# Trainium2 two-block network: all eight residual sums behind out-projection and MLP on VectorE, none on GpSimd

## The chip, the cores and the metric

The program runs on one core of one Trainium2 chip. The time is device microseconds of one whole execution. TensorE (PE in the profile) does the matrix products, VectorE (DVE) and ScalarE (ACT) do elementwise work, GpSimd (POOL) is a fourth engine for elementwise work, and SyncE (SP) issues the transfers. Each engine works through its own queue in order and waits on semaphores for the others.

## What is computed

A first block of two layers works on 512 latent rows and 256 context rows of width 1024, a second block of two layers works on the latent rows alone. Each layer of the first block is a token mixer (Fourier, two kinds of attention, convolution) with an output projection, and an MLP. Behind each of the two stands a gated, normalized residual:

```python
h = _modulate(x, g_pre_mix[l], sx1, cx1)
x = x + gx1 * _rms_norm(_token_mixer(h, kv_ctx, rope, lp, lam, lam_init), g_post_mix[l])
hm = _modulate(x, g_pre_mlp[l], sx2, cx2)
x = x + gx2 * _rms_norm(_sq_relu_mlp(hm, w_ff1[l], w_ff2[l]), g_post_mlp[l])

if l < DEPTH - 1:        # the context, first layer only
    xc = xc + gc1 * _rms_norm(_token_mixer(hc, kv_ctx, None, lp, lam, lam_init), g_post_mix[l])
    hcm = _modulate(xc, g_pre_mlp[l], sc2, cc2)
    xc = xc + gc2 * _rms_norm(_sq_relu_mlp(hcm, w_ff1[l], w_ff2[l]), g_post_mlp[l])
```

So there are six residuals: two of the context (256 columns) and four of the latents (512 columns). The second block has none of this form.

## The kernel before

Activations lie feature-major: `x` (or `context`) is eight tiles f = 0..7 of 128 features by NT columns, NT being 512 or 256, in float32. Every float32 product is made of three passes of split operands (`w_hi`·`h_hi`, `w_hi`·`h_lo`, `w_lo`·`h_hi`, lines 367 to 369 of `Weights.multiply`). ScalarE writes `w_hi` (line 345) and VectorE writes `w_lo` (line 353) of a weight chunk some chunks ahead of its use.

`rest_stage` is what follows the merged branches of a layer: the output projection (eight tiles, evicted to `y`), the norm of y, the residual, the norm in front of the MLP, the MLP in two turns, and again the norm and the residual. It is called for the context of layer 1, the latents of layer 1 and the latents of layer 2. No planner orders it. Each engine has a function, and its order is the order in which that function is written.

One residual (function `residual` on VectorE, line 1413) is this, for f = 0 to 7:

- VectorE scales a tile, `m[f % 4] = y[f] * gain[f] * rows` (line 1420; `m` is called `mid` in the profile, and `rows` is a bank of PSUM with the inverse root for every column).
- The tile is added to x, `x[f] += m[f % 4]`. VectorE adds the tiles 0, 2, 4, 6 and 7 (line 1424), each behind the scaling of the next tile; GpSimd adds the tiles 1, 3 and 5 (line 1403).
- ScalarE squares the new x[f] into `squares[f % 4]` (line 905, called through `RowNorm.square`) for the norm that comes next, `pre_mlp` or `following`.
- TensorE sums four squared tiles at a time (line 913, `RowNorm.sum`, called when f is 3 and when f is 7). ScalarE may square tile 4 only when the first sum is done, since the four buffers are used again.

Two counters say how far the adding is: `rest_added_dve` and `rest_added_pool`. Scaling a tile from f = 4 on waits until tile f - 4 has been added.

Before each sum TensorE runs `keep_busy` products (line 471), 128 by 128 products of constants whose results nobody reads: 32 for 512 columns and 16 for 256, in two runs, one before each sum. In the layer-1 latents' out-projection, `fill` puts products of the modulation (line 2926) in their place. After the second sum come `gather` (VectorE, line 919), `fold` (TensorE, 924), `root` (ScalarE, 930), `invert` (VectorE, 935) and `turn` (TensorE, 940). Then the first products of the MLP may start, or the next stage.

The last residual of the layer-1 context is not done in `rest_stage`. A `LateResidual` object carries it into the input stage of the latents, where its steps are woven among the others' by the marks that each thread yields (`weave_by_clock`: the step with the lowest mark comes next). Its scaling is line 1163, its adding line 1167 on VectorE and line 1174 on GpSimd.

Of the kernel before, what the change touches and what calls it, by code (L numbers as in the profile page):

```python
# [1112 lines left out]
class LateResidual:  # L1113
# [3 lines left out]
    BY_POOL, BY_DVE = (1, 3, 5), (0, 2, 4, 6, 7)  # L1117

    def __init__(self, K, x, y, m, norm, gain, NT, homes):
        self.K, self.x, self.y, self.m, self.norm, self.gain, self.NT, self.homes = K, x, y, m, norm, gain, NT, homes  # L1120
        S = K.count_of
        self.scaled, self.added = S("rest_scaled"), (S("rest_added_dve"), S("rest_added_pool"))

    def wait_added(self, eng, f):
        if f in self.BY_POOL:
            eng.wait_ge(self.added[1].sem, self.added[1].at(self.BY_POOL.index(f) + 1))
        else:
            eng.wait_ge(self.added[0].sem, self.added[0].at(self.BY_DVE.index(f) + 1))

    def wait_all(self, eng):  # L1130
        self.wait_added(eng, self.BY_POOL[-1])
        self.wait_added(eng, self.BY_DVE[-1])
# [17 lines left out]
    def dve(self, dve):  # L1150
# [5 lines left out]
        for f in range(KD + 1):  # L1156
# [8 lines left out]
            if f - 1 in self.BY_DVE:  # L1165
                dve.wait_ge(self.scaled.sem, self.scaled.at(f))
                nc.vector.tensor_tensor(self.x[:, f - 1, 0:NT], self.x[:, f - 1, 0:NT], m[:, (f - 1) % 4], ALU.add)\
                    .then_inc(self.added[0].sem, 1)

    def pool(self, pool):  # L1170
        for f in self.BY_POOL:
            yield 1.0 + 0.15 * f
            pool.wait_ge(self.scaled.sem, self.scaled.at(f + 1))
            self.K.nc.gpsimd.tensor_tensor(self.x[:, f, 0:self.NT], self.x[:, f, 0:self.NT], self.m[:, f % 4], ALU.add)\
                .then_inc(self.added[1].sem, 1)

    def close(self):
        self.norm.close()
        self.scaled.advance(KD)
        self.added[0].advance(len(self.BY_DVE))  # L1180
        self.added[1].advance(len(self.BY_POOL))
# [4 lines left out]
def rest_stage(K, x, merged, mod, mods, NT, following, gates, h, kept, M=None, homes=(), fetch=None, side=None):  # L1186
# [7 lines left out]
    scaled, added = S("rest_scaled"), (S("rest_added_dve"), S("rest_added_pool"))  # L1194
# [13 lines left out]
    with ExitStack() as scope, K.block() as block:  # L1208
# [55 lines left out]
        by_pool = (1, 3, 5)  # L1264
        by_dve = (0, 2, 4, 6, 7)

        def wait_added(eng, turn, f):
            if f in by_pool:
                eng.wait_ge(added[1].sem, added[1].at(len(by_pool) * turn + by_pool.index(f) + 1))
            else:  # L1270
                eng.wait_ge(added[0].sem, added[0].at(len(by_dve) * turn + by_dve.index(f) + 1))
# [126 lines left out]
        @block.gpsimd  # L1398
        def _(pool):
            def residual(turn):  # L1400
                for f in by_pool:
                    pool.wait_ge(scaled.sem, scaled.at(KD * turn + f + 1))
                    nc.gpsimd.tensor_tensor(x[:, f, 0:NT], x[:, f, 0:NT], m[:, f % 4], ALU.add).then_inc(added[1].sem, 1)

            wait_x(pool)
            residual(0)
            if side is None:
                residual(1)

        @block.vector  # L1410
        def _(dve):
            def residual(norm, gain, turn):
# [3 lines left out]
                for f in range(KD + 1):  # L1416
# [5 lines left out]
                    if f - 1 in by_dve:  # L1422
                        dve.wait_ge(scaled.sem, scaled.at(KD * turn + f))
                        nc.vector.tensor_tensor(x[:, f - 1, 0:NT], x[:, f - 1, 0:NT], m[:, (f - 1) % 4], ALU.add)\
                            .then_inc(added[0].sem, 1)
# [7 lines left out]
            wait_added(dve, 0, by_pool[-1])  # L1433
            wait_added(dve, 0, by_dve[-1])
# [32 lines left out]
            if side is None:  # L1467
                residual(post_mlp, mods[:, 3], 1)
                wait_added(dve, 1, by_pool[-1])
# [4 lines left out]
    for s, n in ((scaled, residuals * KD), (added[0], residuals * len(by_dve)), (added[1], residuals * len(by_pool)),  # L1474
# [1298 lines left out]
def input_stage(K, lead, vec, lam, NT, kv, branch, rstd, rope, dft, late=None, late_transfer=None):  # L2773
# [8 lines left out]
    with ExitStack() as scope, K.block() as block:  # L2782
# [79 lines left out]
        def _(pool):  # L2862
            more = [late.pool(pool)] if late is not None else []
            weave_by_clock(fourier.pool(pool), *more)
# [1493 lines left out]
```

## Time and profile before

| | |
|---|---|
| median of 3 runs | 3651.61 us (3648.67 to 3653.59) |
| the profiled execution | 3650.45 us |
| its span, first to last instruction | 3648.7 us |
| TensorE busy | 3458.3 us, 95% |
| VectorE busy | 1906.9 us, 52% |
| ScalarE busy | 1394.7 us, 38% |
| GpSimd busy | 72.5 us, 2% |
| mean granted TensorE clock | 0.978 |

The profiled execution lies 1.16 us below the median, and 1.75 us of it lie outside the span. A busy share is a mean over stages with different limits. What the change meets is six short stretches, which begin at about 382, 591, 1233, 1636, 2359 and 2735 us of the span.

### The profile page before, as it was taken

Reading aid. Unit: us, or ns where it says so; the run is one execution under the profiler, and the core shown is the slowest. Engines: PE = TensorE matmul, PEld = TensorE weight load, DVE = VectorE, ACT = ScalarE, POOL = GpSimd, SP = SyncE. Lnnn points to the kernel's source line nnn. Section 1 sums busy time; section 2 is a strip of 40 time slices with the busy share of each in tenths; the row PEclk is TensorE's granted clock in tenths of the full one; section 3 lists DMA queues with packets and bytes.
Section 4 is the critical chain, followed back from the end, with each engine's and each line's share of the span. In section 5 each row is a group of like instructions: output and inputs, shape, how many; then the busy total and the mean of one; then the engine's idle time right before and its main releaser. Section 6 shows DMA issues by size and latency. Waiting matters only on the chain. (4 is left out here: it accounts for less than half of the span.)

```text
span 3648.7 us, 46697 instructions
## 1 busy us (share of the span) xinstructions
PE 3458.3 (95%) x18528; PEld 2716.4 (74%) x18528; DVE 1906.9 (52%) x3008; ACT 1394.7 (38%) x2383; POOL 72.5 (2%) x58
## 2 busy tenths in 40 slices
PE   7999999999999999998999999999997999989999
PEld 5878898765777677877775677788876776667767
DVE  4655677856544433444856544354443365333653
ACT  4544443344443422224334443322223444343442
POOL 0000000000000000000000000000000000000000
PEclk8999999999999999998999999999998999999999
DMA  5555454211123643323221122223332211222112
GB/s 194 196 192 196 145 185 148 72 56 41 58 64 110 237 164 119 98 87 113 76 70 41 47 67 96 81 82 98 98 93 78 74 60 41 88 92 70 58 41 98
DMA packets 97260, 366.73 MB, mean 101 GB/s; under 512 B 11168, under 2 KB 11424, under 8 KB 95520
## 3 DMA queue, kind: packets, MB, share of 16 engines
q1 hardware_dynamic: 97056, 363.84, 31.0%
q8 instruction: 148, 2.42, 0.3%
q14 instruction: 56, 0.46, 0.0%
HBM read 354.36 MB, written 9.44 MB: 100 GB/s over the span
## 5 line engine op out<-in xcount | busy, mean ns | idle before, releaser
L353 DVE TENSOR_TENSOR w_lo<-w_raw,w_hi 128x1024 fp32r<-128x1024 f32 x545 | 667.7, 1226 | 611.5 <-ACT w_hi L345 611.3
L367 PE MATMUL banks<-h_hi,w_hi 128*128 128x512 f32 (+2 forms) x2040 | 805.6, 395 | 19.4 <-DVE h_lo L1018 6.6
L369 PE MATMUL banks<-h_hi,w_lo 128*128 128x512 f32 (+2 forms) x2040 | 747.8, 367 | 0.0
L368 PE MATMUL banks<-h_lo,w_hi 128*128 128x512 f32 (+2 forms) x2040 | 746.6, 366 | 0.0
L345 ACT ACTIVATE w_hi<-w_raw 128x1024 fp32r<-128x1024 f32 x545 | 573.4, 1054 | 311.0 <-DMA w_raw<-in_stream 299.2
L367 PEld LDWEIGHTS banks<-h_hi,w_hi 128*128 128x128 f32 (+1 forms) x2040 | 392.3, 192 | 123.4 <-issue 53.1
L369 PEld LDWEIGHTS banks<-h_hi,w_lo 128*128 128x128 f32 (+1 forms) x2040 | 390.9, 192 | 64.6
L368 PEld LDWEIGHTS banks<-h_lo,w_hi 128*128 128x128 f32 (+1 forms) x2040 | 392.8, 193 | 58.5 <-issue 10.6
L367 PE MATMUL banks<-merged_hi,w_hi 128*128 128x512 f32 (+1 forms) x960 | 341.1, 355 | 5.0 <-DVE mid L1449 2.3
L369 PE MATMUL banks<-merged_hi,w_lo 128*128 128x512 f32 (+1 forms) x960 | 337.6, 352 | 0.0
L368 PE MATMUL banks<-merged_lo,w_hi 128*128 128x512 f32 (+1 forms) x960 | 337.6, 352 | 0.0
L367 PE MATMUL banks<-mid_hi,w_hi 128*128 128x512 f32 (+1 forms) x768 | 273.8, 356 | 0.5 <-DVE y L1466 0.2
L368 PE MATMUL banks<-mid_lo,w_hi 128*128 128x512 f32 (+1 forms) x768 | 271.6, 354 | 0.0
L369 PE MATMUL banks<-mid_hi,w_lo 128*128 128x512 f32 (+1 forms) x768 | 271.6, 354 | 0.0
L367 PEld LDWEIGHTS banks<-merged_hi,w_hi 128*128 128x128 f32 x960 | 180.2, 188 | 42.8 <-DVE mid L1449 5.9
L1644 ACT ACTIVATE turned<-banks 128x512 f32<-128x512 f32 (+1 forms) x176 | 96.8, 550 | 282.5 <-PE banks L1623 282.5
L369 PEld LDWEIGHTS banks<-merged_hi,w_lo 128*128 128x128 f32 x960 | 180.3, 188 | 25.3
L368 PEld LDWEIGHTS banks<-merged_lo,w_hi 128*128 128x128 f32 x960 | 180.3, 188 | 24.1
L1386 ACT ACTIVATE mid_hi<-mid 128x512 fp32r<-128x512 f32 (+1 forms) x96 | 54.0, 563 | 319.1 <-DVE mid L1449 319.0
L2416 DVE SCALAR_TENSOR_TENSOR branch<-conv_in,vectors,branch 128x512 f32<-128x512 f32 (+1 forms) x270 | 168.2, 671 | 0.2
L367 PEld LDWEIGHTS banks<-mid_hi,w_hi 128*128 128x128 f32 x768 | 145.1, 189 | 30.8 <-issue 4.6
L369 PEld LDWEIGHTS banks<-mid_hi,w_lo 128*128 128x128 f32 x768 | 145.1, 189 | 20.0
(385 smaller groups left out, 4644.2 us busy)
## 6 DMA issues: line engine op xcount, KB each, us to landing
w_raw<-in_stream SPq DMA_DIRECT2D x545, 512.0 KB, 3.6
mod_cells<-in_stream SPq DMA_DIRECT2D x48, 512.0 KB, 5.6
mod_cell<-in_stream SPq DMA_DIRECT2D x48, 512.0 KB, 5.5
x_kept<-x SPq DMA_DIRECT2D x3, 2048.0 KB, 7.2
x<-x_kept SPq DMA_DIRECT2D x3, 2048.0 KB, 8.9
x<-in_x SPq DMA_DIRECT2D x2, 2048.0 KB, 9.7
out_x<-x SPq DMA_DIRECT2D x8, 256.0 KB, 4.5
dft_table<-in_dft SPq DMA_DIRECT2D x2, 768.0 KB, 7.1
```

What stands on the lines that cost most here:

```text
L345: self.nc.scalar.activation(self.hi[:, c], self.raw[:, c], ACT.Copy).then_inc(self.hi_ready, 1)
L353: self.nc.vector.tensor_tensor(self.lo[:, c], self.raw[:, c], self.hi[:, c].bitcast(F32), ALU.subtract)\
L367: self.nc.tensor.matmul(out, w_hi, x_hi, start=start, stop=False)
L368: self.nc.tensor.matmul(out, w_hi, x_lo, start=False, stop=False)
L369: mm = self.nc.tensor.matmul(out, w_lo, x_hi, start=False, stop=stop)
L1386: nc.scalar.activation(mid_hi[:, t], m[:, t % 2], ACT.Copy).then_inc(mid_hi_ready.sem, 1)
L1644: nc.scalar.activation(self.T[:, lane:lane + lanes, a:b, i * P:(i + 1) * P], K.ps[:, 4, 0:lanes * (b - a) * P].rearrange("p (l k n) -> p l ...
L2416: nc.vector.scalar_tensor_tensor(out=self.out[:, c], in0=src, scalar=w, in1=self.out[:, c], op0=ALU.mult, op1=ALU.add).then_inc(self.done. ...
```

## The change

The division of the tiles between the two engines goes. VectorE adds each of the eight tiles, still behind the scaling of the next one. GpSimd's function in `rest_stage` and `LateResidual.pool` go, and one counter is left, `rest_added_dve`. The counts of products, of scalings, of squares and of `keep_busy` products stay, as do their orders.

```diff
-    BY_POOL, BY_DVE = (1, 3, 5), (0, 2, 4, 6, 7)
...
     def wait_added(self, eng, f):
-        if f in self.BY_POOL:
-            eng.wait_ge(self.added[1].sem, self.added[1].at(self.BY_POOL.index(f) + 1))
-        else:
-            eng.wait_ge(self.added[0].sem, self.added[0].at(self.BY_DVE.index(f) + 1))
+        eng.wait_ge(self.added.sem, self.added.at(f + 1))
...
-        @block.gpsimd
-        def _(pool):
-            def residual(turn):
-                for f in by_pool:
-                    pool.wait_ge(scaled.sem, scaled.at(KD * turn + f + 1))
-                    nc.gpsimd.tensor_tensor(x[:, f, 0:NT], x[:, f, 0:NT], m[:, f % 4], ALU.add).then_inc(added[1].sem, 1)
...
-                    if f - 1 in by_dve:
+                    if f >= 1:
                         dve.wait_ge(scaled.sem, scaled.at(KD * turn + f))
                         nc.vector.tensor_tensor(x[:, f - 1, 0:NT], x[:, f - 1, 0:NT], m[:, (f - 1) % 4], ALU.add)\
-                            .then_inc(added[0].sem, 1)
+                            .then_inc(added.sem, 1)
...
             if side is None:
                 residual(post_mlp, mods[:, 3], 1)
-                wait_added(dve, 1, by_pool[-1])
             if following is not None:
                 following.gather(dve)
```

VectorE's queue at the residual behind the out-projection of layer 2 (512 columns; `mid` is m), before:

```order
L1420 SCALAR_TENSOR_TENSOR mid_20607<-y_20604,mods_60,banks 128x512 [waits post_mix_turned]
L1420 SCALAR_TENSOR_TENSOR mid_20607<-y_20604,mods_60,banks 128x512
L1424 TENSOR_TENSOR x_20602<-x_20602,mid_20607 128x512 [waits rest_scaled]
L1420 SCALAR_TENSOR_TENSOR mid_20607<-y_20604,mods_60,banks 128x512 x2
L1424 TENSOR_TENSOR x_20602<-x_20602,mid_20607 128x512 [waits rest_scaled]
L1420 SCALAR_TENSOR_TENSOR mid_20607<-y_20604,mods_60,banks 128x512 [waits rest_added_dve]
L1420 SCALAR_TENSOR_TENSOR mid_20607<-y_20604,mods_60,banks 128x512 [waits rest_added_pool]
```

and with the change:

```order
L1388 SCALAR_TENSOR_TENSOR mid_20596<-y_20593,mods_60,banks 128x512 [waits post_mix_turned]
L1388 SCALAR_TENSOR_TENSOR mid_20596<-y_20593,mods_60,banks 128x512
L1392 TENSOR_TENSOR x_20591<-x_20591,mid_20596 128x512 [waits rest_scaled]
L1388 SCALAR_TENSOR_TENSOR mid_20596<-y_20593,mods_60,banks 128x512
L1392 TENSOR_TENSOR x_20591<-x_20591,mid_20596 128x512 [waits rest_scaled]
L1388 SCALAR_TENSOR_TENSOR mid_20596<-y_20593,mods_60,banks 128x512
L1392 TENSOR_TENSOR x_20591<-x_20591,mid_20596 128x512 [waits rest_scaled]
L1388 SCALAR_TENSOR_TENSOR mid_20596<-y_20593,mods_60,banks 128x512 [waits rest_added_dve]
L1392 TENSOR_TENSOR x_20591<-x_20591,mid_20596 128x512 [waits rest_scaled]
```

The last row shown is the add of tile 3. It was GpSimd's, and needed only the scaling of tile 3 and GpSimd's own add of tile 1. It now stands on VectorE behind five scalings and three adds.

VectorE's queue at the late residual of the context (256 columns), inside the input stage of the latents, before:

```order
L1167 TENSOR_TENSOR context_65<-context_65,mid_4009 128x256 [waits rest_scaled]
L1163 SCALAR_TENSOR_TENSOR mid_4009<-y_4005,mods_60,banks 128x256
L353 TENSOR_TENSOR w_lo_51<-w_raw_49,w_hi_50 128x1024 [waits w_hi_ready]
L1163 SCALAR_TENSOR_TENSOR mid_4009<-y_4005,mods_60,banks 128x256
L1167 TENSOR_TENSOR context_65<-context_65,mid_4009 128x256 [waits rest_scaled]
```

and with the change:

```order
L1161 TENSOR_TENSOR context_65<-context_65,mid_4009 128x256 [waits rest_scaled]
L1157 SCALAR_TENSOR_TENSOR mid_4009<-y_4005,mods_60,banks 128x256
L1161 TENSOR_TENSOR context_65<-context_65,mid_4009 128x256 [waits rest_scaled]
L353 TENSOR_TENSOR w_lo_51<-w_raw_49,w_hi_50 128x1024 [waits w_hi_ready]
L1157 SCALAR_TENSOR_TENSOR mid_4009<-y_4005,mods_60,banks 128x256
L1161 TENSOR_TENSOR context_65<-context_65,mid_4009 128x256 [waits rest_scaled]
```

One add comes in front of the split of a weight chunk (line 353), and the two others in front of the next split.

## Rows read from the trace of the kernel before

**Rows 1.** The page, busy time of TensorE and of GpSimd

```profile
PE 3458.3 (95%) x18528; PEld 2716.4 (74%) x18528; DVE 1906.9 (52%) x3008; ACT 1394.7 (38%) x2383; POOL 72.5 (2%) x58
```

**Rows 2.** Waits, layer-2 out-projection residual, 2359 to 2378 us: total, times, longest

```profile
PE banks L913 <- ACT squares L905: 2.2, 1, 2.2
...
ACT squares L905 <- POOL x L1403: 1.0, 2, 0.5
```

**Rows 3.** Timeline of ScalarE and TensorE there: start, duration, instruction, idle before

```profile
2364.60 0.63 ACT L905 ACTIVATE squares<-x 128x512 f32<-128x512 f32 x1 [0.50 <-POOL x L1403]
...
2365.28 1.07 PE L913 MATMUL banks<-squares,consts 128*32 128x512 f32 x8 [2.24 <-ACT squares L905]
2366.27 3.84 PE L471 MATMUL banks<-consts 128*128 128x128 f32 x32
2370.04 1.06 PE L913 MATMUL banks<-squares,consts 128*32 128x512 f32 x8
```

**Rows 4.** Timeline of VectorE there

```profile
2359.51 1.41 DVE L1420 SCALAR_TENSOR_TENSOR mid<-y,mods,banks 128x512 f32<-128x512 f32 x2 [1.25 <-PE banks L940]
2360.83 0.68 DVE L1424 TENSOR_TENSOR x<-x,mid 128x512 f32<-128x512 f32 x1
2361.43 1.40 DVE L1420 SCALAR_TENSOR_TENSOR mid<-y,mods,banks 128x512 f32<-128x512 f32 x2
...
2371.27 0.69 DVE L919 COPY squares<-banks 128x512 f32<-128x512 f32 x1 [3.40 <-PE banks L913]
```

**Rows 5.** Timeline of GpSimd there

```profile
2362.91 1.66 POOL L1403 TENSOR_TENSOR x<-x,mid 128x512 f32<-128x512 f32 x1 [0.26 <-DVE mid L1420]
```

**Rows 6.** Line 1424 over the run: count, ns min/median/max, first and last start

```profile
L1424 DVE TENSOR_TENSOR x<-x,mid x20: 681/683/686, 1234.6 to 2743.1; 128x512 f32<-128x512 f32 x20
```

**Rows 7.** Timeline of TensorE, first sums of the three other latent residuals

```profile
1239.03 1.07 PE L913 MATMUL banks<-squares,consts 128*32 128x512 f32 x8 [2.24 <-ACT squares L905]
...
1642.13 1.07 PE L913 MATMUL banks<-squares,consts 128*32 128x512 f32 x8 [2.24 <-ACT squares L905]
1643.13 5.47 PE L471 MATMUL banks<-consts 128*128 128x128 f32 x32
...
2741.16 1.07 PE L913 MATMUL banks<-squares,consts 128*32 128x512 f32 x8 [2.24 <-ACT squares L905]
```

**Rows 8.** Timeline of the context's out-projection residual: TensorE, VectorE, ScalarE

```profile
385.79 0.64 PE L913 MATMUL banks<-squares,consts 128*32 128x256 f32 x8 [1.67 <-ACT squares L905]
...
388.34 0.64 PE L913 MATMUL banks<-squares,consts 128*32 128x256 f32 x8
...
382.37 0.87 DVE L1420 SCALAR_TENSOR_TENSOR mid<-y,mods,banks 128x256 f32<-128x256 f32 x2 [0.80 <-PE banks L940]
383.16 0.42 DVE L1424 TENSOR_TENSOR context<-context,mid 128x256 f32<-128x256 f32 x1
383.50 0.86 DVE L1420 SCALAR_TENSOR_TENSOR mid<-y,mods,banks 128x256 f32<-128x256 f32 x2
...
385.32 0.42 ACT L905 ACTIVATE squares<-context 128x256 f32<-128x256 f32 x1 [0.17 <-POOL context L1403]
```

**Rows 9.** Timeline of VectorE at the late residual

```profile
592.78 1.37 DVE L353 TENSOR_TENSOR w_lo<-w_raw,w_hi 128x1024 fp32r<-128x1024 f32 x1
...
598.33 1.23 DVE L353 TENSOR_TENSOR w_lo<-w_raw,w_hi 128x1024 fp32r<-128x1024 f32 x1 [0.88 <-ACT w_hi L345]
```

**Rows 10.** Waits, 590 to 640 us

```profile
PEld banks L367 <- issue: 0.4, 2, 0.2
```

**Rows 11.** Stretches: length, busy PE PEld DVE ACT POOL (instructions), granted clock, DMA share, GB/s

```profile
1240.64:1244.03 3.39, 3.39 (x20) 1.22 (x20) 0.98 (x2) 0.73 (x2) 0.00 (x0) 0.50 1.04 413
1643.42:1646.83 3.41, 3.41 (x18) 3.41 (x18) 1.31 (x3) 2.10 (x4) 0.00 (x0) 0.50 0.00 0
2363.62:2367.03 3.41, 1.75 (x14) 0.91 (x15) 3.41 (x6) 1.66 (x4) 2.60 (x2) 1.00 0.00 0
...
2742.50:2745.91 3.41, 3.41 (x19) 3.41 (x18) 1.25 (x3) 2.04 (x4) 0.00 (x0) 0.50 0.01 2
```

More of the change, by code:

```diff
@@ L1121, in __init__ @@
         S = K.count_of
-        self.scaled, self.added = S("rest_scaled"), (S("rest_added_dve"), S("rest_added_pool"))
+        self.scaled, self.added = S("rest_scaled"), S("rest_added_dve")
     def wait_added(self, eng, f):
-        if f in self.BY_POOL:
-            eng.wait_ge(self.added[1].sem, self.added[1].at(self.BY_POOL.index(f) + 1))
-        else:
-            eng.wait_ge(self.added[0].sem, self.added[0].at(self.BY_DVE.index(f) + 1))
+        eng.wait_ge(self.added.sem, self.added.at(f + 1))
     def wait_all(self, eng):
-        self.wait_added(eng, self.BY_POOL[-1])
-        self.wait_added(eng, self.BY_DVE[-1])
+        self.wait_added(eng, KD - 1)
     def pe(self, pe):
@@ L1164, in dve @@
                                                op0=ALU.mult, op1=ALU.mult).then_inc(self.scaled.sem, 1)
-            if f - 1 in self.BY_DVE:
+            if f >= 1:
                 dve.wait_ge(self.scaled.sem, self.scaled.at(f))
                 nc.vector.tensor_tensor(self.x[:, f - 1, 0:NT], self.x[:, f - 1, 0:NT], m[:, (f - 1) % 4], ALU.add)\
[L1168 to L1175, printed above, removed]
+                    .then_inc(self.added.sem, 1)
     def close(self):
@@ L1179, in close @@
         self.scaled.advance(KD)
-        self.added[0].advance(len(self.BY_DVE))
-        self.added[1].advance(len(self.BY_POOL))
+        self.added.advance(KD)
         for t in self.homes:
@@ L1193, in rest_stage @@
     S = K.count_of
-    scaled, added = S("rest_scaled"), (S("rest_added_dve"), S("rest_added_pool"))
+    scaled, added = S("rest_scaled"), S("rest_added_dve")
     up_free, down_free, mid_hi_ready, mid_lo_ready = S("mlp_up_bank_free"), S("mlp_down_bank_free"), S("mlp_mid_hi"), S("mlp_mid_lo")
@@ L1262, in wait_x @@
                 eng.wait_ge(x_in.sem, x_in.at(16))
-        by_pool = (1, 3, 5)
-        by_dve = (0, 2, 4, 6, 7)
         def wait_added(eng, turn, f):
[L1268 to L1271, printed above, removed]
+            eng.wait_ge(added.sem, added.at(KD * turn + f + 1))
         beside_pe = None
@@ L1396, in _ @@
                 following.root(act)
-        @block.gpsimd
-        def _(pool):
-            def residual(turn):
-                for f in by_pool:
-                    pool.wait_ge(scaled.sem, scaled.at(KD * turn + f + 1))
-                    nc.gpsimd.tensor_tensor(x[:, f, 0:NT], x[:, f, 0:NT], m[:, f % 4], ALU.add).then_inc(added[1].sem, 1)
[L1405 to L1408, printed above, removed]
         @block.vector
@@ L1432, in _ @@
             residual(post_mix, mods[:, 1], 0)
[L1433 to L1434 removed]
+            wait_added(dve, 0, KD - 1)
             lead.dve(dve, True, range(up + AHEAD, up + SLOTS))
@@ L1473, in rest_stage @@
     residuals = 2 if side is None else 1
-    for s, n in ((scaled, residuals * KD), (added[0], residuals * len(by_dve)), (added[1], residuals * len(by_pool)),
+    for s, n in ((scaled, residuals * KD), (added, residuals * KD),
                  (K.dve_step, 8 * turns), (up_free, 8 * turns),
@@ L2862, in _ @@
         def _(pool):
-            more = [late.pool(pool)] if late is not None else []
-            weave_by_clock(fourier.pool(pool), *more)
+            weave_by_clock(fourier.pool(pool))
         @block.vector
```

1 line of the change is left out of this document (added).

## The prediction, made before the changed kernel ran

> **What bounds the kernel now.** The page comes first: TensorE is busy for 95% of the span and GpSimd for 2% [rows 1]. What lengthens the program is what lengthens TensorE's queue, so the question at each of the six residuals is whether TensorE waits there, and for whom.
>
> I read the waits of one residual, then its instructions in order of time. At the out-projection of layer 2, TensorE waits 2.24 us for ScalarE's squares before the first sum, and ScalarE waits twice for GpSimd's adds [rows 2, 3]. In order of time the chain is: GpSimd adds tile 3 from 2362.91 for 1.66 us; ScalarE squares it from 2364.60, 0.03 us after the add has ended; the sum starts at 2365.28 [rows 3, 5]. So the end of GpSimd's add of tile 3 sets the first sum. From there TensorE doesn't wait: 32 products that keep it busy run from 2366.27, and the second sum follows them at 2370.04 [rows 3]. VectorE, done with its adds by then, waits 3.40 us for that sum [rows 4]. The other three latent residuals show the same 2.24 us before their first sum [rows 7], the context's out-projection shows 1.67 us [rows 8].
>
> **VectorE's spacing.** From 2359.51 to 2360.83 there are two scalings, so one takes 0.66 us of the queue; an add takes 0.60 (2360.83 to 2361.43) and ends 0.68 after its start [rows 4]. For 256 columns the same differences give 0.395 for a scaling and 0.34 for an add, which ends 0.42 after its start [rows 8]. The changed queue alternates the same two instructions, each still one instruction behind what it needs, and the scaling of tile 4 needs the add of tile 0, long done. I let no new wait in.
>
> **First sum, four latent residuals.** The add of tile 3 now stands behind five scalings and three adds of VectorE: 5 x 0.66 + 3 x 0.60 = 5.10 us after 2359.51, that is 2364.61, and ends at 2365.29. The square then starts at 2365.32 and no longer at 2364.60: 0.72 us later. Nothing covers this, since TensorE is the one that waits; its gap grows from 2.24 to 2.96 us. Four times 0.72 is 2.88 us.
>
> **Second sum.** The added work here is three adds, 1.8 us of VectorE's queue, and it is covered. The add of tile 7 starts after 8 x 0.66 + 7 x 0.60 = 9.48 us, at 2368.99, ends at 2369.67, its square (0.63) ends at about 2370.34 and the sum could start at 2370.38. TensorE gets there by its own products at 2370.04 + 0.72 = 2370.76. The cover is 0.38 us; were it gone, each residual would cost what the adds exceed it by. The gather behind it has more: VectorE is free at 2369.67, the gather stood at 2371.27 [rows 4].
>
> **Context, out-projection.** The add of tile 3 starts 5 x 0.395 + 3 x 0.34 = 3.00 us after 382.37, ends at 385.79, and the square starts at 385.82 where it started at 385.32: 0.50 us. The second sum is a tie: TensorE's side gives 388.34 + 0.50 = 388.84, VectorE's side 382.37 + 5.54 + 0.42 + 0.42 + 0.08 = 388.83. I take 0.50, with 0.1 more as the bound.
>
> **Late residual of the context.** Three adds of 0.34 are 1.02 us more on VectorE, and behind them stand the splits of weight chunks. Before the split at 598.33 VectorE waited 0.88 us for ScalarE [rows 9], so it comes about 0.14 us late, and the one before by 0.34. The waits of this stretch hold none of TensorE's for a split, only 0.4 us of issue [rows 10]. I cost it at nothing; the cover is that weights are split chunks ahead, and all of it on the path would be 1.02 us. The transfer of the context waits for one counter instead of two and is issued long after.
>
> **GpSimd leaving.** It loses 12 adds of 1.66 us and six short ones. No queue behind them holds anything that TensorE needs at once, so this gives nothing by itself. Could VectorE have been held by GpSimd? Its 20 adds of 512 columns take 681 to 686 ns, some of them beside GpSimd's and the last two of each residual without it [rows 6], and the two scalings that run beside a GpSimd add take 1.40 us together where the two before any took 1.41 [rows 4]. I see nothing to win back in the residuals. One place looks different: the split at 592.78, while GpSimd's first late add ran, took 1.37 us and the one at 598.33 took 1.23 [rows 9]. That 0.14 us lies on a covered queue.
>
> The Trainium skill (SBUF — State Buffer, section "Who interferes with whom") says that a VectorE instruction with two SBUF inputs and a GpSimd instruction that reads SBUF exclude each other, and that the one that issues first blocks the other for its whole length. The long split agrees with it; by that rule taking GpSimd away could shorten VectorE's chain, and the sum would be smaller wherever GpSimd had come first. In the residuals the adds of 681 to 686 ns show that it didn't.
>
> **The sum.** 2.88 + 0.50 + 0 = 3.38 us on the profiled execution's 3650.45 us, or 3653.83. The median of the runs stands 1.16 higher, at 3651.61, so the forecast is 3655.0 us, 0.09% more.
>
> **The clock, the largest unknown.** In three of the four latent residuals the granted clock falls to 0.50 for about 3.4 us right behind the first sum, in the fourth it stays at 1.00, though the gap of 2.24 us is the same [rows 7, 11]. 0.50 is 1.2 GHz, 1.00 is 2.4 GHz. What a fall costs is read from the 32 products: 5.47 us with it against 3.84 without [rows 7, 3], so 1.63 us. The skill (TensorE: Matmul & The Clock Gate, Part 1) says that the gate looks at activity in windows that run freely, whatever the kernel does; the same gap with and without a fall agrees with that. What a gap of 2.96 us does no row shows.
>
> **The rivals.**
>
> (a) *The delay as summed*, 3.4 us: about 3655.0, with its own range of 3652.5 to 3657.5. For it speaks that the wait before the first sum is there five times, almost alike. Chance 0.55.
>
> (b) *The clock gives a part back.* Where the clock falls and returns at moments of its own, work that starts 0.72 us later spends 0.72 us less in the stretch of half speed, and half of the delay returns: 0.36 in three residuals, so 0.50 + 0.72 + 3 x 0.36 = 2.3 us, 3653.9. If one or two of the three falls are also missed because everything has shifted, 1.63 us go off each time: 3652.3 or 3650.6. For it speaks that one residual has no fall; against it that a longer gap makes none less likely. Chance 0.22.
>
> (c) *The clock falls in the two places where it doesn't now*, the layer-2 out-projection and the context's: 3.4 + 2 x 1.63 = 6.6 us, 3658.3. For it: the gaps grow by 0.72 and 0.50. Chance 0.14.
>
> (d) *The other side, slower by over 0.2%*: the longer gap brings half speed not for one stretch but for a second as well, at the five first sums. Each further stretch costs up to 1.63. It decides from three further stretches on, 3.4 + 4.9 = 8.3 us, 3659.9; with five it is 3.4 + 8.2 = 11.6 us, 3663.2. Against it: in all three falls seen, the clock is back when the products after the sum end. Chance 0.07.
>
> (e) *VectorE runs faster alone*, as the shared port would have it. To lose nothing at the first sum, the nine instructions up to the end of tile 3's add would have to take 5.06 us where I sum 5.78, an eighth less. Then the time stays at about 3651.6, and only a gain beyond that is faster. Chance 0.02.
>
> **How the numbers follow.** The likeliest is (a), 3655.0. The range of 3650.0 to 3661.0 holds (a), (b), (c) and the beginning of (d), and some 2 us by which the median of a few runs may lie off (the three runs shown span 4.9 us). Within 0.2%, which is 7.3 us and about what a measurement can tell from no change, lie (a), (b), (c) and (e): 0.91 after the unlikely tail of (b) and (e) below 3644.3 is taken at 0.01 or 0.02. Slower takes (d) and a corner of (c), 0.08; faster 0.01.
>
> **What would show it.** In the changed profile TensorE's wait before the first sum should be 2.9 to 3.0 us at the four latent residuals and about 2.2 at the context's, with VectorE's add of tile 3 ending 0.03 before the square. The distance from the first to the second sum should stay 4.76 us where the clock stays, and the second sum should still show no wait. VectorE's spacing should be 0.66 and 0.60. GpSimd's busy time should fall by some 25 us. I am wrong if the second sum waits for ScalarE (the cover of 0.38 was none), if the first sum isn't later (the chain was another), or if the stretches behind the first sums show a clock of 0.50 more often or longer than three times 3.4 us.

## The result

The changed kernel takes 3663.65 us (median of 9 runs, 3657.05 to 3673.28), the kernel before beside it 3655.13 us (9 runs, 3648.67 to 3656.73). The ratio is 1.0027, with a 95% interval of 1.0019 to 1.0036: slower by 7 to 13 us. A second set of 10 runs, in the last but one group of experiments, gives 3662.60 beside 3654.12, 1.0019 (1.0010 to 1.0029). The forecast was 3655.0 with a range up to 3661.0, so it was wrong: the 3.4 us were there, and 3.5 to 6.5 us more stood beside them. Of the 8.7 us between the forecast and the median, 3.5 are the kernel before itself: its median was 3651.61 in the three runs that the forecast was built on, and 3655.13 in these nine.

From here on the places have letters: A is the residual behind the context's out-projection (at about 382 us before), C and D are the two of layer 1's latents, behind the out-projection (1233) and behind the MLP (1636), E and F the same of layer 2 (2359 and 2735). B is the late residual of the context (591).

The page of the profiled execution (3667.31 us, mean granted clock 0.975 where it was 0.978), span and busy times, which answers to [rows 1]:

```profile
span 3665.5 us, 46692 instructions
PE 3469.8 (95%) x18528; PEld 2721.8 (74%) x18528; DVE 1915.2 (52%) x3026; ACT 1395.9 (38%) x2383; POOL 48.2 (1%) x40
```

GpSimd is 24.3 us shorter and 18 instructions lighter. VectorE has those 18 instructions and 8.3 us more. What the queue of TensorE shows is new: the same 18528 matmuls keep it busy 11.5 us longer. Its work didn't grow, it ran slower. Summed over the clock's stretches in the two traces, the granted clock stood at 0.50 for 184.6 us where it stood there for 160.7. At half speed half of such time is lost, 12.0 us of the 23.9.

Place E in order of time, VectorE, ScalarE, then TensorE (start, duration, instruction, idle before it in brackets); it answers to [rows 3, 4]:

```profile
2372.77 1.41 DVE L1388 SCALAR_TENSOR_TENSOR mid<-y,mods,banks 128x512 f32<-128x512 f32 x2 [1.25 <-PE banks L940]
2374.10 0.68 DVE L1392 TENSOR_TENSOR x<-x,mid 128x512 f32<-128x512 f32 x1
2374.70 0.74 DVE L1388 SCALAR_TENSOR_TENSOR mid<-y,mods,banks 128x512 f32<-128x512 f32 x1
2375.36 0.68 DVE L1392 TENSOR_TENSOR x<-x,mid 128x512 f32<-128x512 f32 x1
...
2377.88 0.68 DVE L1392 TENSOR_TENSOR x<-x,mid 128x512 f32<-128x512 f32 x1
...
2378.59 0.63 ACT L905 ACTIVATE squares<-x 128x512 f32<-128x512 f32 x1 [0.63 <-DVE x L1392]
...
2379.27 1.07 PE L913 MATMUL banks<-squares,consts 128*32 128x512 f32 x8 [2.97 <-ACT squares L905]
2380.27 5.47 PE L471 MATMUL banks<-consts 128*128 128x128 f32 x32
2385.67 1.06 PE L913 MATMUL banks<-squares,consts 128*32 128x512 f32 x8
```

The spacing of VectorE is 0.60 and 0.66 us. The add of tile 3 begins 5.11 us after the first scaling and ends at 2378.56, the square starts 0.03 later, and TensorE waits 2.97 us instead of 2.24. All of this is as summed. The next row of TensorE isn't: the 32 filler matmuls behind the first sum take 5.47 us where they took 3.84 [rows 3].

The same two or three rows of TensorE at A, C, D and F, which answer to [rows 7, 8]:

```profile
389.60 0.64 PE L913 MATMUL banks<-squares,consts 128*32 128x256 f32 x8 [2.14 <-ACT squares L905]
390.17 3.51 PE L471 MATMUL banks<-consts 128*128 128x128 f32 x16
393.61 0.76 PE L913 MATMUL banks<-squares,consts 128*32 128x256 f32 x8
...
1246.37 1.13 PE L913 MATMUL banks<-squares,consts 128*32 128x512 f32 x8 [2.97 <-ACT squares L905]
1247.43 1.87 PE L2903 MATMUL banks<-consts,mod_rows 128*128 128x2 f32 x8
1249.23 3.64 PE L2891 MATMUL banks<-mod_cell,cond_silu 128*32 128x512 f32 x16
...
1257.75 1.03 PE L913 MATMUL banks<-squares,consts 128*32 128x512 f32 x8
...
1653.34 1.91 PE L913 MATMUL banks<-squares,consts 128*32 128x512 f32 x8 [2.97 <-ACT squares L905]
1655.18 4.62 PE L471 MATMUL banks<-consts 128*128 128x128 f32 x32
...
2756.76 1.94 PE L913 MATMUL banks<-squares,consts 128*32 128x512 f32 x8 [2.97 <-ACT squares L905]
2758.63 5.79 PE L471 MATMUL banks<-consts 128*128 128x128 f32 x32
2764.35 1.06 PE L913 MATMUL banks<-squares,consts 128*32 128x512 f32 x8
```

And the stretches of half speed behind the five first sums, A, C, D, E, F (length, busy time of PE, PEld, DVE, ACT and POOL with their instructions, granted clock, share of the DMA engines, GB/s), which answer to [rows 11]:

```profile
390.50:393.90 3.40, 3.40 (x20) 3.08 (x22) 1.11 (x4) 1.34 (x4) 0.00 (x0) 0.50 0.01 2
1247.25:1257.48 10.23, 10.23 (x52) 4.93 (x52) 2.79 (x5) 2.86 (x5) 0.00 (x0) 0.50 0.97 358
1653.43:1656.84 3.41, 3.41 (x16) 1.75 (x16) 3.41 (x6) 1.48 (x3) 0.00 (x0) 0.50 0.02 5
2380.47:2383.88 3.41, 3.41 (x17) 3.41 (x17) 2.47 (x5) 2.49 (x4) 0.00 (x0) 0.50 0.01 2
2755.94:2762.76 6.82, 6.00 (x27) 4.33 (x28) 4.49 (x8) 2.90 (x5) 0.00 (x0) 0.50 0.01 4
```

Before, three of the five places had one stretch each. Now all five have one, F for 6.82 us and C for 10.23. At C the matmuls that run at half speed are the modulation's own work, not filler. From the first sum to the second it takes 4.01 us at A, 11.38 at C, 6.4 at D, 6.40 at E and 7.59 at F. Before it was 2.55 at A (388.34 - 385.79), 4.76 at E, 6.4 at D and F (1.00 to the products and 5.47 for them), and 8.2 at C.

**Where the 16.8 us between the spans of the two profiled executions lie.** I laid the two traces side by side by the same instruction of VectorE, place by place. The changed one is later by 2.0 us at A, 3.9 at C, 0.7 at D, 2.3 at E and 1.9 at F, 10.8 in all. 3.3 us had been there by 380 us, before any instruction that the change touches, and 2 to 3 us come and go in unchanged code between the places. So this pair of profiles shows the mechanism but overstates the loss; the ratios of the two sets give 7 to 10, the medians 8.5 in both.

### The profile page after: what moved, and what is told of

The parts are those of the page before. It is cut to its first block and busy times, and to the rows that moved or that the text cites. A ratio compares the mean times of both kernels' runs of the same rounds, so it can differ in the third digit from the quotient of the medians.

```text
span 3665.5 us, 46692 instructions
## 1 busy us (share of the span) xinstructions
PE 3469.8 (95%) x18528; PEld 2721.8 (74%) x18528; DVE 1915.2 (52%) x3026; ACT 1395.9 (38%) x2383; POOL 48.2 (1%) x40
## 5 line engine op out<-in xcount | busy, mean ns | idle before, releaser
L368 PEld LDWEIGHTS banks<-h_lo,w_hi 128*128 128x128 f32 (+1 forms) x2040 | 393.5, 193 | 58.9 <-issue 10.8
L368 PEld LDWEIGHTS banks<-merged_lo,w_hi 128*128 128x128 f32 x960 | 180.3, 188 | 24.3
```

What stands on the lines that cost most here:

```text
L368: self.nc.tensor.matmul(out, w_hi, x_lo, start=False, stop=False)
```

## The experiments

In the list, "ratio" is to the kernel before, measured on the same chip with it, with its 95% interval. 0.0001 of it is 0.37 us.

### 1. Which tiles matter

`e1_pool_1_3` gives only tile 5 to VectorE, `e2_pool_5` only the tiles 1 and 3. The late residual is split in the same way in both.

```diff
 e1:
-        by_pool = (1, 3, 5)
-        by_dve = (0, 2, 4, 6, 7)
+        by_pool = (1, 3)
+        by_dve = (0, 2, 4, 5, 6, 7)
 e2:
+        by_pool = (5,)
+        by_dve = (0, 1, 2, 3, 4, 6, 7)
```

> GpSimd keeps the adds of tiles 1 and 3, VectorE takes the add of tile 5 beside its five. Theory (gap: the first sum comes later, TensorE's gap before it grows, and the clock falls more often behind it): the first sum still waits for GpSimd's add of tile 3, so the gap stays 2.24 us and the time stays that of the kernel before, within 2 us of 3655. Rival (the loss lies in the second half of the adds, or in VectorE's longer queue as such): a third of the loss shows, 3658.

> The other half: VectorE adds tiles 1 and 3, GpSimd keeps tile 5 alone. Gap theory: the first sum is as late as in the changed kernel, gap 2.96 us at the latents, so the time is the changed kernel's, 3661 to 3664. Rival (it is GpSimd's absence, or the second sum): 3655 to 3658.

Measured: e1 1.0005 (0.9996 to 1.0014), e2 1.0022 (1.0013 to 1.0031), both as the gap theory expected. The loss is that of tiles 1 and 3, of what stands ahead of the first sum. Tile 5, behind it, costs nothing that shows.

### 2. Filling the gap

If half speed behind the first sum is the missing part, it should go when TensorE has something to do in the gap. A call `K.keep_busy(pe, n, 0)` with n filler products was put ahead of the first sum.

```diff
+                if f == 3:
+                    K.keep_busy(pe, 24 if NT == SEQ else 16, 0)
                 pre_mlp.sum(pe, f)
```

That is `e3_after_filled` (on the changed kernel, and the same ahead of `following.sum`); `e4_before_filled` has 18 and 12 on the kernel before.

> The changed kernel with 24 more products of constants in front of each first sum (16 for 256 columns), which fill TensorE's gap of 2.97 us (2.14) nearly; everything else as in the changed kernel. Gap-and-clock theory: the granted clock no longer falls right behind the first sums of the residuals, and what is left is the later sums, 3.4 us, less the falls that the kernel before had there too, so 3651 to 3657. Rival (all 8.5 us are time on the path, and the clock has no part): the time stays at 3663.

> The kernel before with 18 more products of constants in front of each first sum (12 for 256 columns), which fill its gap of 2.24 us (1.67). Gap-and-clock theory: the falls behind the first sums go, three of 1.63 us in the profile, so about 3650. Rival (the clock has no part): 3655, no change.

Measured: e3 1.0027 (1.0017 to 1.0036), e4 1.0018 (1.0009 to 1.0027). Neither came out as expected, and the reason is a miscount of mine. One product of `keep_busy` shows as two matmuls in the trace. (So the prediction's "32 products" behind the first sum are 16 products and 32 matmuls; no term of its sum depends on it.) Place E of e3:

```profile
2364.38 9.10 PE L471 MATMUL banks<-consts 128*128 128x128 f32 x80
2373.41 1.07 PE L913 MATMUL banks<-squares,consts 128*32 128x512 f32 x8
2374.40 3.84 PE L471 MATMUL banks<-consts 128*128 128x128 f32 x32
```

48 matmuls more last 5.4 us where the gap was 3, and the sum starts some 2.4 us after the last square it needs (ScalarE had ended it at 2371.03). But the 3.84 behind it says that the clock stays. So I halved the numbers: `e5_after_filled_12` has 12 (8 for the context) on the changed kernel, `e6_before_filled_9` has 9 (6) on the one before, at the same two lines.

> The changed kernel with 12 more products in front of each first sum (8 for 256 columns). A product shows as two matmuls in the trace, so this is half of what e3 added: 24 x 0.1175 = 2.8 us in a gap of 2.97 us, 1.9 in 2.14; it must not delay the sum. Theory (gap and clock: the 8 to 10 us are 3.4 us of later sums and the rest half speed behind longer gaps): no half speed behind the first sums, time at or below before + 3.4, that is a ratio of 0.9995 to 1.001. Rival (the clock is not what costs; time goes on the path elsewhere): ratio 1.0027 as for the changed kernel.

> The kernel before with 9 more products in front of each first sum (6 for 256 columns): 18 matmuls of 0.1175 are 2.1 us in a gap of 2.24. Theory: the three to five falls behind its first sums go, 0.5 to 1.63 us each, ratio 0.9985 to 0.9995. Rival (clock without a part): ratio 1.000.

Measured: e5 3650.75 us, 0.9991 (0.9982 to 1.0000); e6 3647.23 us, 0.9982 (0.9973 to 0.9991). Place E of e5, then of e6:

```profile
2361.14 6.42 PE L471 MATMUL banks<-consts 128*128 128x128 f32 x56
2367.84 1.07 PE L913 MATMUL banks<-squares,consts 128*32 128x512 f32 x8 [0.29 <-ACT squares L905]
2368.84 3.84 PE L471 MATMUL banks<-consts 128*128 128x128 f32 x32
```

```profile
2360.41 5.75 PE L471 MATMUL banks<-consts 128*128 128x128 f32 x50
2366.40 1.07 PE L913 MATMUL banks<-squares,consts 128*32 128x512 f32 x8 [0.24 <-ACT squares L905]
2367.39 3.84 PE L471 MATMUL banks<-consts 128*128 128x128 f32 x32
```

Both kernels now keep the clock behind all five first sums. They differ by what the change does and by the gap's filling, which leaves both with 0.2 to 0.35 us of gap where there is one, and their mean granted clock over the eleven runs is the same, 0.979. The difference is 3.5 us, give or take 2.0 by the spread of the runs, which agrees with the 3.4 us of later first sums. The change itself stands 0.0028 to 0.0036 above e5, 10 to 13 us, though its first sums begin no later than e5's. The kernel before stands 6.6 us above e6. What is left of the change beyond its 3.4 us is the difference of these two.

### 3. A shorter gap by another order

`e7_order` leaves GpSimd the tiles 1 and 5, and moves VectorE's adds so that tile 3 is ready sooner:

```diff
+                for step, f in ((scale, 0), (scale, 1), (add, 0), (scale, 2), (scale, 3), (add, 2), (add, 3), (scale, 4),
+                                (scale, 5), (add, 4), (scale, 6), (scale, 7), (add, 6), (add, 7)):
+                    step(f)
```

`e8_order_filled` adds 7 filler products (5 in the context) ahead of the first sum and cuts the run ahead of the second from 16 to 11 (8 to 6).

> GpSimd adds tiles 1 and 5 only; VectorE adds tile 3, but right behind the add of tile 2 and ahead of the scaling of tile 4: four scalings and two adds stand in front of it, 4 x 0.66 + 2 x 0.60 + 0.68 = 4.52 us, where the kernel before took 5.06. The gap shrinks from 2.24 to 1.70 (latents) and from 1.67 to 1.44 (context). Theory (the length of the gap sets time and clock): faster than before by 4 x 0.54 + 0.23 = 2.4 us and by some falls, ratio 0.998 to 0.9993. Rival (VectorE's adding of tile 3 itself is what costs): slower than before.

> e7's order, with 7 more products in front of the first sum (5 for 256 columns) and 11 instead of 16 in front of the second one (6 instead of 8). The squares of the second half end some 1.3 us before the products do, so TensorE's own products hold the second sum. Theory: another 1.2 us at three latent residuals and 0.4 at the context's over e7, and no falls behind the first sums: ratio 0.9965 to 0.998. Rival (fewer products let the clock fall): no better than e7.

Measured: e7 3648.59 us, 0.9992 (0.9982 to 1.0001), with a gap of 1.71 us at D, E and F and of 1.42 at A; e8 3646.06 us, 0.9982 (0.9973 to 0.9991). The first sum is 0.53 us earlier at three places, 0.38 at C and 0.25 at A, 2.2 us in all, and e7's ratio is worth 2.9, in an interval that just reaches zero. e8 is better by 3.7 us more, a little less than was expected. In e8's trace the second sum of E waits 0.72 us for ScalarE, so the second run was cut too short.

### 4. The gap's length alone, the late residual alone, the best of it, and the change once more

`e9_before_less` makes the gap of the kernel before as long as the change makes it, without moving any sum: 13 filler products instead of 16 ahead of the first sum at D, E and F, 6 instead of 8 at A. At C the modulation's products fill, and stay.

```diff
-                    fill(pe, 4, busy, 0)
+                    fill(pe, 4, busy if f == 7 else (13 if NT == SEQ else 6), 0)
-                        K.keep_busy(pe, busy, 0)
+                        K.keep_busy(pe, busy if f == 7 else 13, 0)
```

`e10_late_only` gives VectorE all adds of the late residual (B) and nothing else. `e11_order_filled_14` is e8 with 6 (5) products in the gap and 14 (7) ahead of the second sum. `e12_after_again` is the changed kernel.

> The kernel before with 3 products fewer (6 matmuls, 0.70 us) in front of the first sum at the three latent residuals that have such products, and 2 fewer (0.47 us) at the context's. The gap grows to 2.94 and 2.14 us as in the changed kernel, but VectorE, GpSimd and the moment of the first sum stay. Theory (the length of the gap alone brings half speed): slower than before by 2 to 6 us, ratio 1.0006 to 1.0016, with half speed behind more of these sums. Rival (it takes the later sum, or VectorE's longer queue): ratio 1.000.

> Only the late residual of the context gives GpSimd's three adds to VectorE; the five others stay as before. The prediction costed this part at nothing: ratio 1.000 within 0.0008. Rival (the delayed splits reach TensorE, up to 1.0 us, or shift the stage behind): ratio 1.0003 to 1.001.

> e8 with 6 products in front of the first sum and 14 in front of the second (7 at the context), since e8's profile shows 0.72 us of waiting before the second sum and none before the first. TensorE should wait 0.2 us before the first and none before the second sum. Theory: as e8 or 1 us better by less half speed, ratio 0.9975 to 0.9985. Rival (products have nothing left to give): as e8.

> The changed kernel once more, in the same call as the three others, so that they are read against the same runs of before. Both theories: ratio 1.002 to 1.0035. Its profile shows whether half speed behind the first sums is the rule or one execution's: theory, at least five of the gaps' stretches, as in the first profile.

Measured: e9 1.0002 (0.9993 to 1.0011), e10 1.0002 (0.9992 to 1.0011), e11 3644.97 us, 0.9973 (0.9964 to 0.9982), e12 1.0019 (1.0010 to 1.0029). e10 shows no cost of B, though its interval allows 4 us; what speaks for none is that neither its profile nor the changed one has any wait of TensorE from 595 to 660 us. e11 is the best version: 9 us under the kernel before, 18 under the changed one in the same group.

e9 went against my theory as I had put it. Here are its first sums at D, E and F:

```profile
1650.33 1.06 PE L913 MATMUL banks<-squares,consts 128*32 128x512 f32 x8 [2.91 <-ACT squares L905]
1651.32 3.84 PE L471 MATMUL banks<-consts 128*128 128x128 f32 x32
...
2374.03 1.06 PE L913 MATMUL banks<-squares,consts 128*32 128x512 f32 x8 [2.91 <-ACT squares L905]
2375.03 3.84 PE L471 MATMUL banks<-consts 128*128 128x128 f32 x32
...
2749.69 1.06 PE L913 MATMUL banks<-squares,consts 128*32 128x512 f32 x8 [2.91 <-ACT squares L905]
2750.69 3.84 PE L471 MATMUL banks<-consts 128*128 128x128 f32 x32
```

The gap is 2.91 us, as good as the changed kernel's, and the clock falls behind none of the three. So the length of the gap alone isn't what brings half speed there. At A it looks otherwise. There e9's gap is 2.11 us with the sum where it was, and the 16 matmuls behind it take 3.03 us instead of 2.05:

```profile
388.06 0.64 PE L913 MATMUL banks<-squares,consts 128*32 128x256 f32 x8 [2.11 <-ACT squares L905]
388.63 3.03 PE L471 MATMUL banks<-consts 128*128 128x128 f32 x16
```

 In e9 the gap begins earlier and ends where it ended before; in the changed kernel it begins where it did and ends 0.72 us later.

### 5. Which places: the change and its filling, split

e9 left open whether the rest was at C, which it didn't touch. Four kernels split the question in two ways. e13 and e14 make the change in a part of the places, on the kernel before (B as before in both):

```diff
-        by_pool = (1, 3, 5)
-        by_dve = (0, 2, 4, 6, 7)
+        by_pool = () if M is not None else (1, 3, 5)
+        by_dve = tuple(f for f in range(KD) if f not in by_pool)
```

`M is not None` holds in layer 1's latents (C, D); `e14_all_but_layer_1` has `M is None` there (A, E, F). e15 and e16 are e5 with the filling in a part of the places:

```diff
-                if f == 3:
+                if f == 3 and M is not None:
                     K.keep_busy(pe, 12 if NT == SEQ else 8, 0)
```

and `M is None` in `e16_fill_all_but_layer_1`, the same ahead of `following.sum`.

> The kernel of before with all eight additions on VectorE in the latent stage of layer 1 alone, behind its out-projection and behind its MLP (the two places called C and D here); the context stage, layer 2 and the late residual stay as before. Path term by the prediction: 2 x 0.72 = 1.4 us. Theory 1 (the 5 us that the change loses beyond its 3.4 us lie behind the first sum of layer 1's out-projection, where the products that fill the gap are the modulation's own work and three stretches at 0.50 stood after the change where the kernel before had one): 1.4 + 5 = 6.5 us over before, ratio 1.0018. Rival (they are spread over all five places, by how long the gap ahead of the first sum is): 1.4 + 2 = 3.4 us, 1.0009. Second rival (they lie in the context stage and in layer 2): 1.4 us, 1.0004.

> The complement: all eight additions on VectorE in the context stage and in layer 2 (A, E and F), layer 1's latent stage and the late residual as before. Path term 0.50 + 2 x 0.72 = 1.9 us. Theory 1 (the rest is in layer 1): 1.9 us over before, ratio 1.0005. Rival (spread by places): 1.9 + 3 = 4.9 us, 1.0013. Second rival (all of it here): 1.9 + 5 = 7 us, 1.0019.

> The changed kernel with 12 filler products (24 matmuls) more ahead of the first sum in the latent stage of layer 1 alone (C and D), the other places as changed. All filled gave 3650.8 beside a kernel before of 3653.4, and the change alone 8.5 us over before: the fill is worth 11 us in all. Theory 1: what the change lost at C comes back with what before itself loses there, 5 + 2 to 3 of the 11 us: about 1 us over before, ratio 1.0003. Rival (spread): 4 to 5 of the 11 us, 4 us over before, 1.0011.

> The complement: the changed kernel with 12 filler products more (8 in the context stage) ahead of the first sum at A, E and F, layer 1 as changed. Theory 1: 3 to 4 of the 11 us come back, 5 us over before, ratio 1.0013. Rival (spread): 6 to 7 of the 11 us, 2 us over before, 1.0005.

Measured: e13 1.0011 (0.9999 to 1.0023), e14 1.0009 (1.0000 to 1.0018), e15 1.0006 (0.9997 to 1.0015), e16 1.0005 (0.9997 to 1.0014). By the ratios the parts are 4.0 and 3.3 us, 7.3 together, about what the whole loses (the medians, 6.0 and 6.1 us over before, would make it 12); either half of the filling brings 5 to 8 us of e5's 10 to 13. Theory 1, that C holds the rest, gave 1.0018, 1.0005, 1.0003 and 1.0013 for the four; the spread gave 1.0009, 1.0013, 1.0011 and 1.0005. Neither series is met in all four. The halves come out alike, which fits a spread over both better, but all four intervals hold both values. What decides is the rows, which follow the edit place by place. In e13, C (changed) and E (unchanged):

```profile
1238.77 1.06 PE L913 MATMUL banks<-squares,consts 128*32 128x512 f32 x8 [2.97 <-ACT squares L905]
1239.77 1.48 PE L2940 MATMUL banks<-consts,mod_rows 128*128 128x2 f32 x8
1241.18 3.64 PE L2928 MATMUL banks<-mod_cell,cond_silu 128*32 128x512 f32 x16
...
2371.78 1.07 PE L913 MATMUL banks<-squares,consts 128*32 128x512 f32 x8 [2.23 <-ACT squares L905]
2372.78 3.84 PE L471 MATMUL banks<-consts 128*128 128x128 f32 x32
```

In e14, C (unchanged) and E (changed):

```profile
1246.41 1.07 PE L913 MATMUL banks<-squares,consts 128*32 128x512 f32 x8 [2.24 <-ACT squares L905]
...
1248.53 3.42 PE L2928 MATMUL banks<-mod_cell,cond_silu 128*32 128x512 f32 x16
...
1252.86 1.92 PE L2928 MATMUL banks<-mod_cell,cond_silu 128*32 128x512 f32 x16
...
2376.61 1.07 PE L913 MATMUL banks<-squares,consts 128*32 128x512 f32 x8 [2.97 <-ACT squares L905]
2377.61 5.47 PE L471 MATMUL banks<-consts 128*128 128x128 f32 x32
```

**All profiles together.** One row as these can be read at D, E and F of each kernel, by whether it takes 4.8 us (clock kept) or 6.3 and more (fallen) from the first sum to the second. The kernels e3, e4, e8 and e11, in which the counts of filler differ, are left out:

| gap before the first sum | kernels | places | clock falls behind it |
|---|---|---|---|
| 2.96 to 2.97 us, sum 0.72 later | changed, e12, e2 (D, E, F); e14, e15 (E, F); e13, e16 (D) | 15 | 14, four of them (F) for twice as long |
| 2.23 to 2.24 us | before, e1, e10 (D, E, F); e13 (E, F); e14 (D) | 12 | 4 |
| 2.91 us, sum as before | e9 | 3 | 0 |
| 1.71 us | e7 | 3 | 0 |
| 0.2 to 0.3 us | e5, e6 (D, E, F); e15 (D); e16 (E, F) | 9 | 0 |

At C the clock is at 0.50 for 10.2 us behind the gap of 2.97 us in five profiles of five (changed, e2, e12, e13, e16); behind the gap of 2.24 us for 3.4 us in four (before, e9, e10, e14) and for 10.2 in one (e1); behind e7's gap, which is 1.86 us at C, for 3.4; and not at all behind the filled gap in three (e5, e6, e15). The one exception of the first line is F of e2, where the products take 3.84 us behind a gap of 2.96. At A the clock falls behind the gap in all four profiles with 2.11 to 2.15 us (changed, e2, e9, e14) and in none of the three with 1.66 to 1.67 (before, e10, e13). In e1, e12 and e15 it had fallen there ahead of the gap, in the products that precede it, which leaves a gap of 0.76 to 1.18 us and no fall behind it.

**The moment of the first sum.** The gap leaves cases unsorted: 4 of 12, 0 of 3 in e9, the exceptions F of e2 and C of e1. The same profiles sort them by one more number. The five stretches of the changed profile above begin 856.75, 406.18, 727.04 and 375.47 us apart, which is 251, 119, 213 and 110 times the shortest of them. In each of the 18 profiles all stretches of half speed begin whole numbers of that shortest stretch apart, to 0.01 us. So one can tell from the stretches elsewhere in a profile at which moments its clock could have fallen behind a sum where it didn't. In e9, counted on from the stretch at C (first row), such a moment comes 2.09 us behind the first sum of D, and the clock stays (second row):

```profile
1246.23:1249.64 3.41, 3.41 (x18) 0.64 (x17) 0.68 (x2) 0.43 (x1) 0.00 (x0) 0.50 1.02 417
1652.42:1655.83 3.41, 3.41 (x33) 2.71 (x31) 0.50 (x1) 1.29 (x3) 0.00 (x0) 1.00 0.00 0
```

Here are the 42 places of the table once more (D, E and F), by the time from the start of the first sum to the next such moment:

| next moment behind the start of the sum | gap | places | clock falls |
|---|---|---|---|
| 0.00 to 1.43 us | 2.96 to 2.97 us | 10 (D, E) | 10 |
| 2.59 to 2.81, the one before it inside the gap, 0.61 to 0.83 ahead of the sum | 2.97 | 4 (F) | 4, from that one on, twice as long |
| 2.15 | 2.96 | 1 (F of e2) | 0 |
| 0.22 to 1.55 | 2.24 | 4 | 4 |
| 1.59 to 2.09 | 2.23 to 2.24 | 8 | 0 |
| 1.82 to 2.09 | 2.91 (e9) | 3 | 0 |
| 1.86 to 2.65 | 1.71 (e7) | 3 | 0 |
| 0.29 to 2.11 | 0.2 to 0.3 | 9 | 0 |

With a gap of 2.2 us and more the moment sorts every one of the 30 cases. It sorts C too: 10.2 us of half speed in the six profiles with 0.78 to 1.53 us to the next moment, the one of e1 among them, and 3.4 us in the five with 1.61 to 1.93. And it says what the change did. At C the next moment is 1.53 to 1.93 us away in the profiles with the old sum, and 0.78 to 1.45 in those whose sum starts 0.72 us later; e9, whose sum isn't later, stays at 1.82 to 2.09 at D, E and F. That the gap counts beside the moment is shown by the filled ones: five of the nine have 0.29 to 1.52 us, and none has a fall. At A the two can't be told apart: the four profiles with a fall have 0.90 to 1.43 us, the three without 1.52 to 2.02. All this is read off after the runs, from one profile of each kernel; none of them moved a sum and held its gap.

## Why the prediction was wrong

**The chain to the first sum, right.** The gap is 2.97 us at the four latent places (summed: 2.96) and 2.14 at A (2.17). VectorE keeps its spacing, and nothing new waits. The 3.38 us agree with the difference of e5 and e6, 3.5 us (1.5 to 5.5), which have the same mean clock.

**The second sum, right.** No second sum waits in the changed profile, but the cover of 0.38 us was never put to the test at E and elsewhere, since the half speed ahead of the second sum made TensorE later than VectorE by more. VectorE waits 3.93 us for it at E, where it waited 3.40 [rows 4]:

```profile
2386.87 0.69 DVE L919 COPY squares<-banks 128x512 f32<-128x512 f32 x1 [3.93 <-PE banks L913]
```

In e5, where the clock stays, the second sum of E starts at 2372.61 without a wait, 0.44 us after the last square has ended (2372.17), so the cover does hold.

**The late residual, right.** e10 puts it at 0.7 us, in an interval from 3 us less to 4 us more, and TensorE waits for nothing there.

**GpSimd leaving, right.** No gain shows. The adds on VectorE take what they took [rows 6]:

```profile
L1392 DVE TENSOR_TENSOR x<-x,mid x32: 678/681/684, 1241.2 to 2759.7; 128x512 f32<-128x512 f32 x32
```

The one row that had looked different did change: the split of weights among the late residual's steps took 1.37 us [rows 9] and takes 1.22 now, like its neighbour.

```profile
599.76 1.22 DVE L353 TENSOR_TENSOR w_lo<-w_raw,w_hi 128x1024 fp32r<-128x1024 f32 x1
```

The Trainium skill (SBUF — State Buffer, section "Who interferes with whom") says that a VectorE instruction with two SBUF inputs, as this split is, contends with a GpSimd instruction that reads SBUF. The 0.15 us agree with it in sign, and they lie on a queue with cover.

**The clock, wrong, and this is the step that failed.** The sum has no term for it: half speed was to stay as it was, in three stretches of 3.4 us. The changed profile has 27.3 us of it behind the five first sums instead of 10.2, which is one of the signs of being wrong that the prediction names. I had both halves of what came as rivals. (c), "The clock falls in the two places where it doesn't now", had 0.14, and it fell at E and at A. (d), "the longer gap brings half speed not for one stretch but for a second as well", had 0.07, and there are three further stretches, two at C and one at F. The two together are 3.4 + 3.3 + 4.9 = 11.6 us by the prediction's prices, where the five places of the pair of profiles show 10.8. So the prices were about right and the chances were the mistake. The one reason against (d) was that "in all three falls seen, the clock is back when the products after the sum end", which was read off falls behind a gap of 2.24 us and says nothing of another. And I took the falls for chance, "the same gap with and without a fall", where the moment of the sum, which the change puts 0.72 us later, tells them apart. The profile of before held a hint of it: the next moment is 1.28 and 1.34 us behind the start of the sum at D and F, where the clock falls, and 1.76 at E, where it doesn't.

How far it goes: from 4 of 12 to 14 of 15 at D, E and F, which is (14/15 - 4/12) x 1.63 x 3 = 2.9 us. F's longer stretch adds 1.2 to 1.3 (7.59 to 7.70 against 6.39) in four profiles of five. At C 11.38 against 8.2 is 3.2 us, and one of the five profiles with a gap of 2.24 had that already. A adds 1.0 to 1.5 in the three profiles of five in which it falls behind the gap. That is 6 to 8 us, an estimate, on top of 3.4. The ratios leave 3.5 to 6.5 on top, so up to some 4 us must come back elsewhere. A piece of it can be seen behind E: the changed profile is 2.3 us later there by the residual and 0.7 us less late by 2430, since the kernel before had a fall in the work that follows (16 filler matmuls in 2.89 us) and the changed one didn't (1.95). I can't account for all of it.

**C, the largest single loss.** I had counted it as one of three falls, and in the profile of before it is one: it takes 8.18 us from the first sum to the second, and 6.56 where the clock stays (e5), so the fall costs 1.62 there as elsewhere. Behind the later sum half speed stayed for 10.23 us, and C lost 3.9 us in the pair of profiles. Its stretch isn't filled with products of constants but with the modulation's. Nothing in the rows of before showed that it would stay three times as long.

**What stays open.** The Trainium skill (TensorE: Matmul & The Clock Gate, Part 1) says that the gate's windows run freely and don't start with the kernel. The profiles agree: the first of the moments at which the clock can fall comes anywhere from 0.01 to 3.23 us after the first instruction. Yet at one place the later sum stands much alike to them from profile to profile, 0.00 to 0.57 us ahead of the next at D and 0.75 to 1.43 at E; why, no run here tells. Nor does one tell whether a gap of 2.24 us and one of 2.97 differ at the same moment, since both fell wherever the next one was at most 1.43 us away. Why C keeps half speed longer than the others isn't shown either: its products are another kind and DMA is busy there (358 GB/s), and no run separates the two.

## What to carry to other kernels

When a change makes TensorE wait longer at some place, the wait can be the smaller part of the price if the granted clock there is already seen to fall now and then. Price the fall (here 1.63 us on 3.84), and look at where the falls stand: in this kernel 0.72 us more turned 4 falls in 12 into 14 in 15, and the falls went with the moment at which the work resumed, while the same gap without the later start (e9) brought none at three places and one at a fourth. And try the filler: 12 products in a gap of 3 us were worth 10 to 13 us of 3663, more than the change cost, as long as they end before the data is there.

## What the runs showed of the hardware

- Half speed behind a gap needn't begin with the work. At E of the changed profile the sum ran its 1.07 us at full speed and the clock fell 1.20 us after its start, at C of the one before 1.61 after. At F it fell 0.83 us ahead of the sum, inside the gap.
- The stretches of half speed of one profile begin whole numbers of the shortest stretch apart (18 profiles, to 0.01 us), and behind a gap of 2.2 to 3 us it was the sum's place between two such moments that went with the fall, in 30 cases of 30.
- Most of what one execution differs by from the next goes with the clock: the nine runs of the changed kernel go from 3655.3 us of span at a mean clock of 0.977 to 3671.5 at 0.974, and over the 32 to 35 runs of before in each group 0.001 of mean clock goes with some 3 us.
- A product of two float32 operands of 128 by 128, as `keep_busy` issues it, shows as two matmuls of about 0.115 us each (56 in 6.42 us at E of e5). A count of filler by the source is half of the count in the trace.
